# Changed places of modulation passes, attention values and an up-projection in a two-block transformer kernel

## The chip, the cores and the metric

The kernel is one program on one core of one Trainium2 chip. Its time is the device time of one launch in microseconds (us). The core has a matrix engine, TensorE (PE in the rows; PEld is its weight load), VectorE (DVE), ScalarE (ACT), GpSimd (POOL) and SyncE (SP), whose queue issues most loads. The engines run their own instruction streams and meet at semaphores.

## The reference

Two transformer blocks in float32 on 256 tokens of width 1024. The change lies in the first block:

```python
mod = silu(c) @ ada_w + ada_b                       # 6 * 1024 values
shift1, scale1, gate1, shift2, scale2, gate2 = split(mod, 6)
u = rms_norm(x, norm1_g) * (1 + scale1) + shift1
q_a, kc, vc, ksl, vsl, kwn, vwn, g_a, q_b, k_b, v_b, m_a, m_b = split(u @ w_in)
q_a = rms_norm(q_a per head, q_norm_g)
y_a = nsa_attention(q_a, ...) @ w_up_nsa            # 8 heads: compressed, selected, window
y_b = stick_breaking_attention(q_b, k_b, v_b) @ w_up_sb   # 8 heads
h = x + gate1 * ((sigmoid(m_a) * y_a + sigmoid(m_b) * y_b) @ w_out)
h = h + gate2 * (square(relu((rms_norm(h) * (1 + scale2) + shift2) @ mlp_w1)) @ mlp_w2)
```

Stick breaking weighs a key by `exp(log_sigmoid(z) + suffix sum of log_sigmoid(-z))`. The second block (SwiGLU, spatial gating, latent and memory attention, SwiGLU) isn't touched.

## The kernel before

All weights come as one stream of 128x128 chunks, eight to a slot of 512 KB, in the order in which PE uses them (`stream_chunks`). SP loads slots into a ring of six; a slot is loaded again when PE has given it back. Each slot is used in two parts for precision: ACT rounds it into one of four halves (`round_slot`, L1363), then DVE subtracts the rounded from the full value in place (`split_slot`, L1809). Neither has a queue for that of its own: `ahead(name)` stands in their programs and works up to four slots past the slot in which PE makes `name`. A projection (`project`, L685 through `mm`) makes a block of 128 outputs for 256 tokens: per 128 rows of weights three matmuls, so 24 for a full block over 1024 rows and 12 for a half one.

PSUM has eight banks. `plan_psum` gives each named result a bank, in turn within a list of names; `claim` makes PE wait until the result before in that bank has been read, and `full` and `evacuated` are the other engines' waits. `proj_names` and `later_proj_names` use banks 0 to 2 in rotation, `long_names` bank 7, and `selection_names` lists its banks one by one.

The order in time around the change is the order in which each engine's program is written. PE: the first projections; `ga`, `ks`, `kw`, `qa0` to `qa3`, each with the sum of squares of the one before; the compression of keys and values (`cmp_hid_k`, `cmp_hid_v`, narrow matmuls); the scores of the first two stick-breaking heads; eight times a gate block `ma0` to `ma7` with one stick-breaking head (`sb_logits(h)`), and after every second the values of a pair of heads (`sb_values(b)`, result `sbo0` to `sbo3`); then eight times a gate block `mb0` to `mb7` with the turning (transpose) of one head's weights (`nsa_turn(i)`, L1005), scores and values of pairs (`nsa_scores`, `nsa_values`); then the up-projections `up_nsa0`, `up_sb0` and so on with the memory keys, the mixing (`mix0` to `mix7`), the memory values and the first hidden block.

DVE has at the query norms: `ada_step`, `normalise("qa0")`, and so on for four blocks. `normalise` (L1838) reads the bank of a query block and so frees it: `qa3` holds bank 2, which `ma0` needs. At the compression it multiplies (`cmp_turned`, L1975) what ACT's tanh (L1523) gives, and frees bank 0 for `ma1`. In the gate blocks it makes a head's logits with the bias (`nsa_logits`, L2011), and after ACT's exponentials (`exps`, L1555) scales them (`nsa_scale`, L2030 to L2035). `split_output` (L1824 and L1825) reads an attention output in two parts. ACT loads a table set (`ACT_TABLE_LOAD`) where the kind of function changes.

A modulation pass (`ada_step`, L1865) multiplies 128 rows of `ada_w` (512 KB) by `silu(c)` and sums along the row: one block of 128 values of `mod`. 16 early passes make `shift1` and `scale1`; 32 follow in the order `gate1`, `shift2`, `scale2`, `gate2`. POOL loads their weights into a ring of three (`load_ada`, L1269), the next when a pass is done, from a queue in which it also loads the bias, stores the rounded memory rows (two times 1 MB) and loads them back. `ADA_BEFORE_SB`, `ADA_SB` (per stick-breaking head), `ADA_IN_UP` and `ADA_IN_MIX` say where the 32 passes stand in DVE's program. `gate1` must be ready for the mixing, `shift2` and `scale2` after it.

The weights of the gate blocks' heads lie in two buffers, `logit[:, 0]` and `logit[:, 1]` (`wide[:, 24:28]` and `wide[:, 28:32]`), an odd head in the first. The stick-breaking buffers are `sbw`, `wide[:, 16:28]`: an even head in the first six blocks, an odd one in the last six.

## Time and profile before

| | us |
|---|---|
| three runs | 1054.4, 1056.98, 1057.65 |
| median | 1056.98 |
| profiled execution, its own time | 1056.08 |
| its span, first to last instruction | 1054.4 |
| busy: PE, DVE, ACT, POOL | 1028.0, 806.0, 617.4, 49.2 |

The span and the execution's own time differ by 1.7 us, which lie around the kernel. A timeline row gives start, duration, engine, line, operation, what it writes and reads, how many instructions are merged, and in square brackets idle time of that engine just before, with the line that ended it. An average over the span says little here: PE is busy almost always, and what can be won are single stops of it.

### The profile page before, as it was taken

What the parts mean: (1) busy time and instruction counts of PE and PEld (TensorE: products, weight loads), DVE (VectorE), ACT (ScalarE), POOL (GpSimd) and SP (SyncE); (2) the same over time, 40 slices, a digit from 0 to 9 for tenths busy, and PEclk for the clock granted to TensorE, in tenths of its full rate; (3) what the DMA queues carried; (4) which work ended last, traced back from release to release, by engine and by line L of the source; (5) the groups of instructions that cost most, each with busy time, mean ns of one, the idle gap of its engine ahead of it and who ended that gap; (6) DMA issues with size and microseconds to landing.
All of it is one profiled execution on the core that took longest, in us unless ns stands there. A gap on an engine that the chain in (4) does not pass through costs nothing.

```text
span 1054.4 us, 18897 instructions
## 1 busy us (share of the span) xinstructions
PE 1028.0 (97%) x6878; PEld 932.6 (88%) x6878; DVE 806.0 (76%) x1480; ACT 617.4 (59%) x1147; POOL 49.2 (5%) x74
## 2 busy tenths in 40 slices
PE   6997989999999999999999999999999999999998
PEld 5997978998988888888888889899999998888887
DVE  6987877886998655588887878576867878888753
ACT  5485778545665544466655367696654466555532
POOL 1001100001110000000000010000000020000000
PEclk9998999999999999999999999999999999999999
DMA  9988763668776666666666664455444555666663
GB/s 363 403 313 303 231 206 123 196 196 271 273 224 191 189 189 191 181 185 194 184 195 186 185 187 151 154 147 173 124 138 125 167 170 180 186 193 186 193 185 117
DMA packets 58507, 209.46 MB, mean 199 GB/s; under 512 B 7055, under 2 KB 8463, under 8 KB 57912
## 3 DMA queue, kind: packets, MB, share of 16 engines
q1 hardware_dynamic: 52616, 185.24, 56.1%
q0 software_dynamic: 5808, 23.09, 6.2%
q8 instruction: 55, 0.90, 0.3%
q14 instruction: 28, 0.23, 0.1%
HBM read 205.14 MB, written 3.16 MB: 198 GB/s over the span
## 4 chain that ended last, share of the span: by engine, by line
PE 87%; DVE 5%; ACT 4%; DMA 2%; issue 1%; POOL 0%; ACTq 0%; DVEq 0%; SPq 0%; POOLq 0%
PE bank L685 86%; DVE ring_rounded L1809 2%; ACT rounded_rounded L1363 2%; DMA ada_ring<-in_ada 1%; DMA ring<-in_stream 1%; PE bank L1005 1%; ACT body L1555 1%; DMA x<-in_x_t 0%; DVE ada_ring L2124 0%; DVE body L2035 0%; ACT body_rounded L1412 0%; DVE part L2353 0%; DVE x L2094 0%; DVE x L2165 0%; DVE x L2164 0%
## 5 line engine op out<-in xcount | busy, mean ns | idle before, releaser
L685 PE MATMUL bank<-u_rounded,rounded_rounded 128*128 128x256 f32 (+1 forms) x2136 | 510.4, 331 | 6.4 <-DVE qa L1838 4.7
L1809 DVE TENSOR_TENSOR ring_rounded<-ring,rounded_rounded 128x1024 fp32r<-128x1024 f32 x326 | 397.2, 1225 | 119.0 <-ACT rounded_rounded L1363 112.5
L1363 ACT ACTIVATE rounded_rounded<-ring 128x1024 fp32r<-128x1024 f32 x326 | 341.9, 1054 | 103.2 <-PE bank L685 80.4
L685 PE MATMUL bank<-u_rounded,ring_rounded 128*128 128x256 f32 x1504 | 351.0, 281 | 0.0
L685 PEld LDWEIGHTS bank<-u_rounded,rounded_rounded 128*128 128x128 f32 x2136 | 332.7, 189 | 11.7 <-DVE qa L1838 4.9
L685 PE MATMUL bank<-body_rounded,rounded_rounded 128*128 128x256 f32 (+1 forms) x1296 | 321.9, 335 | 2.1 <-DVE body_rounded L2063 1.3
L685 PEld LDWEIGHTS bank<-u_rounded,ring_rounded 128*128 128x128 f32 x1504 | 284.2, 189 | 37.9
L685 PE MATMUL bank<-body_rounded,ring_rounded 128*128 128x256 f32 x952 | 217.2, 280 | 0.0
L685 PEld LDWEIGHTS bank<-body_rounded,rounded_rounded 128*128 128x128 f32 x1296 | 201.4, 188 | 4.2 <-DVE body_rounded L2063 1.7
L685 PEld LDWEIGHTS bank<-body_rounded,ring_rounded 128*128 128x128 f32 x952 | 178.9, 188 | 26.4
L1616 ACT ACTIVATE part<-bank 128x256 f32<-128x256 f32 x65 | 24.9, 384 | 81.1 <-PE bank L685 81.1
L1865 DVE CUSTOM_DVE_ANT_0 ada_ring<-ada_ring,ada_acc,cols 128x1024 f32<-128x1024 f32 x38 | 48.3, 1280 | 5.2 <-DMA ada_ring<-in_ada 5.2
L1312 POOL TENSOR_TENSOR turned<-turned 128x256 f32<-128x256 f32 x20 | 19.9, 995 | 575.8 <-ACT turned L1639 376.1
L2140 DVE TENSOR_TENSOR part<-bank,part 128x256 f32<-128x256 f32 x65 | 27.6, 424 | 18.4 <-ACT part L1616 18.4
L1555 ACT ACTIVATE body<-body,stats 128x128 f32<-128x128 f32 (+2 forms) x64 | 25.9, 406 | 18.0 <-DVE stats L2327 15.4
L1616 ACT ACTIVATE body<-bank 128x256 f32<-128x256 f32 x44 | 16.8, 382 | 33.1 <-PE bank L685 33.1
L1593 ACT ACTIVATE body_rounded<-body 128x256 fp32r<-128x256 f32 x76 | 31.2, 411 | 8.1 <-DVE body L2218 3.9
L2067 DVE TENSOR_TENSOR body_rounded<-body,body_rounded 128x256 fp32r<-128x256 f32 x76 | 31.8, 419 | 1.1 <-ACT body_rounded L1593 1.0
L685 PE MATMUL bank<-rounded_rounded,u_rounded 128*128 128x512 f32 (+1 forms) x96 | 28.6, 370 | 3.6 <-DVE u_rounded L1907 3.6
L2140 DVE TENSOR_TENSOR body<-bank,body 128x256 f32<-128x256 f32 x44 | 18.7, 424 | 14.6 <-ACT body L1616 14.6
L685 PE MATMUL bank<-body,mats 128*128 128x256 f32 (+1 forms) x82 | 19.8, 382 | 5.6 <-ACT body L1399 5.6
L1269 POOL DMA_DIRECT2D ada_ring<-in_ada x32 | 17.1, 534 | 152.1 <-DVE mod L1865 151.2
(268 smaller groups left out, 883.0 us busy)
## 6 DMA issues: line engine op xcount, KB each, us to landing
ring<-in_stream SPq DMA_DIRECT2D x328, 512.0 KB, 4.2
ada_ring<-in_ada POOLq DMA_DIRECT2D x32, 512.0 KB, 5.1
body<-in_ada SPq DMA_DIRECT2D x8, 512.0 KB, 9.4
ada_ring<-in_ada SPq DMA_DIRECT2D x6, 512.0 KB, 8.4
mem_parts_kept<-body_rounded POOLq DMA_DIRECT2D x2, 1024.0 KB, 7.0
body_rounded<-mem_parts_kept POOLq DMA_DIRECT2D x2, 1024.0 KB, 5.8
x<-in_x_t SPq DMA_DIRECT2D x2, 512.0 KB, 4.8
body<-in_mem_t SPq DMA_DIRECT2D x2, 512.0 KB, 7.1
```

Source lines behind the costliest of these rows:

```text
L685: return nc.tensor.matmul(out, lhs, rhs, start=start, stop=stop, skip_group_check=True)
L1005: return nc.tensor.transpose(ps[:, at_col:at_col + P], src, mat("ident"))
L1269: pool.dma_start(ada_ring[:, n % ADA_RING, :], ada[ADA_EARLY + n]).then_inc(ada_full[n % ADA_RING], 16)
L1312: ins = pool.tensor_tensor(row_squares[:, i, :], row_squares[:, i - 1, :], row_squares[:, i, :], ALU.add)
L1363: a(R(slot_round(q)), slot_weights(n), ACT.Copy).then_inc(slot_rounded, 1)
L1555: ins = a(dst, src, ACT.Exp, scale=-1.0 if i < 8 else 1.0, bias=stats[:, i % 2, 0, k:k + 1], accum_out=stats[:, i % 2, 1, k:k + 1])
L1593: a(R(hidden[:, i, :]), hidden_lo[:, i, :], ACT.Copy).then_inc(hidden_rounded, 1)
L1616: a(dst, bank(name)[:, T:2 * T], ACT.Copy).then_inc(half_copied, 1)
L1809: v.tensor_tensor(R(w), w, R(slot_round(q)), ALU.subtract).then_inc(slot_split, 1)
L1865: v.tensor_tensor_reduce(out=w, in0=w, in1=c_row, scale=0.5, scalar=col("ada_b", at), op0=ALU.mult, op1=ALU.add, accum_out=mod[:, at:at + ...
L2067: v.tensor_tensor(R(hidden_lo[:, i, :]), hidden_lo[:, i, :], R(hidden[:, i, :]), ALU.subtract).then_inc(hidden_ready, 1)
L2140: free(v.tensor_tensor(dst, bank(name)[:, 0:T], dst, ALU.add), name)
```

## The change

The results and the counts of all kinds of work stay as they are; the order and three places in memory change.

- Modulation passes: two stand before the split of the slots at `ks` (`ADA_IN_KEYS`), three before `qa0`, `qa1` and `qa2`, none before `qa3` and none behind it; one less in stick-breaking head 6 (14 passes before the up-projections instead of 16); one more in the up-projections and one more in the mixing. POOL issues the first two reloads ahead of the memory rows' stores.
- The last stick-breaking values (`sb_values(3)`) come behind `mb0`; their result goes to bank 1 instead of 7.
- DVE makes the logits of heads 0 and 1 in a row, before head 0's scaling. ACT takes head 0's exponentials ahead of stick-breaking head 7's, and its table load stands before the copy of `ma7`. Odd heads' weights go to `wide[:, 16:20]`.
- `up_sb0` comes before the last head's turn, its chunks are first in the stream, and `up_sb0` and `up_nsa0` use banks 0 and 2, `up_nsa1` bank 1.

```diff
@@ -52,8 +52,8 @@
 ADA_EARLY = 16
-ADA_SB = (2, 1, 1, 2, 1, 2, 1, 0)
-ADA_BEFORE_SB, ADA_IN_UP, ADA_IN_MIX = 6, (0, 2, 4), (0, 1, 2, 5, 6)
+ADA_SB = (2, 1, 1, 2, 1, 2, 0, 0)
+ADA_IN_KEYS, ADA_BEFORE_SB, ADA_IN_UP, ADA_IN_MIX = 2, 5, (0, 2, 4, 6), (0, 1, 2, 4, 5, 6)
 ADA_UP = ADA_BEFORE_SB + sum(ADA_SB) + ADA_RING
@@ -129,8 +129,11 @@
     for m in range(KD):
+        if m == 0:
+            stationary("w_up_sb", span(m * P), half)
         stationary("w_up_nsa", span(m * P), [span(b * HD, HD) + span((4 + b) * HD, HD) for b in range(4)])
-        stationary("w_up_sb", span(m * P), half)
+        if m:
+            stationary("w_up_sb", span(m * P), half)
         if m % 2 == 0:
@@ -286,8 +289,8 @@
 def later_proj_names():
-    out = []
-    for m in range(KD):
+    out = ["up_sb0", "up_nsa1", "up_nsa0", "up_sb1"]
+    for m in range(2, KD):
         out += [f"up_nsa{m}", f"up_sb{m}"]
@@ -316,7 +319,7 @@
-    out = [("sbz6", 1), ("sbz7", 2), ("ma5", 0), ("ma6", 0), ("ma7", 0)]
+    out = [("sbz6", 1), ("sbz7", 2), ("sbo3", 1), ("ma5", 0), ("ma6", 0), ("ma7", 0)]
     for i in range(8):
@@ -341,7 +344,7 @@
 def long_names():
-    return ["mem_ss", "qa1"] + [f"sbo{b}" for b in range(4)]
+    return ["mem_ss", "qa1"] + [f"sbo{b}" for b in range(3)]
@@ -455,6 +458,7 @@
         logit = flat(wide[:, 24:32, :]).rearrange("p (a b) -> p a b", a=2)
+        nsa_weights = [flat(wide[:, 28:32, :]), flat(wide[:, 16:20, :])]
@@ -1006,7 +1010,7 @@
                 pe.wait_ge(weights_ready, i + 1)
-                w = logit[:, 1 - i % 2, :]
+                w = nsa_weights[i % 2]
                 for t, c in enumerate("sw"):
@@ -1052,12 +1056,19 @@
                     nsa_scores(0)
+            project("mb0", KD, u_parts)
             sb_values(3)
+            def up_sb(m):
+                project(f"up_sb{m}", 4, (attn_b, attn_b_lo1), (lambda i: evacuated(pe, f"sbo{i}")) if m == 0 else None)
+
             for i in range(8):
-                project(f"mb{i}", KD, u_parts)
+                if i:
+                    project(f"mb{i}", KD, u_parts)
                 if i and i % 2 == 0:
                     nsa_values(i // 2 - 1)
+                if i == 7:
+                    up_sb(0)
                 nsa_turn(i)
@@ -1068,8 +1079,9 @@
                     sum_squares(f"mem_k{m // 2}", "ones")
-                project(f"up_sb{m}", 4, (attn_b, attn_b_lo1), (lambda i: evacuated(pe, f"sbo{i}")) if m == 0 else None)
-                if m == 0:
+                if m:
+                    up_sb(m)
+                else:
                     pe.wait_ge(loaded["mem_back"], 32)
@@ -1286,6 +1298,7 @@
                            ).then_inc(loaded["bias"], 16)
+            load_ada(ADA_RING, ADA_RING + ADA_IN_KEYS)
             pool.wait_ge(u_rounded, (ROW_MEM + 1) * KD)
@@ -1294,7 +1307,7 @@
                 pool.tensor_copy(bias_cmp[:, :, t, 0:seen], backwards(bias, (seen - 1) * CMP_STRIDE, seen, CMP_STRIDE)).then_inc(lines_ready, 1)
-            load_ada(ADA_RING, ADA_UP)
+            load_ada(ADA_RING + ADA_IN_KEYS, ADA_UP)
@@ -1511,9 +1524,27 @@
+            def exps(i, parts):
+                if i < 8:
+                    ahead(f"nsa{i}a")
+                    evacuated(act, f"nsa{i}a")
+                else:
+                    ahead(f"mla{i - 8}")
+                    act.wait_ge(logits_ready, i - 8 + 1)
+                for k, (src, dst) in parts.items():
+                    ins = a(dst, src, ACT.Exp, scale=-1.0 if i < 8 else 1.0, bias=stats[:, i % 2, 0, k:k + 1], accum_out=stats[:, i % 2, 1, k:k + 1])
+                ins.then_inc(weights_raw, 1)
+
+            def nsa_exp(i):
+                w = nsa_weights[i % 2]
+                at = [w[:, 0:128], w[:, 128:256], w[:, 256:512], w[:, 512:768], w[:, 768:768 + N_CMP], w[:, 784:784 + N_CMP]]
+                exps(i, {k: (s, s) for k, s in enumerate(at)})
+
             act.wait_ge(mem_stored, 32)
             sb_log(0)
             for h in range(8):
+                if h == 7:
+                    nc.scalar.preload_act_table_set("exp_and_others")
                 copy(gates[:, h, :], f"ma{h}")
@@ -1541,27 +1572,10 @@
                     sb_log(h + 1)
+                else:
+                    nsa_exp(0)
                 sb_exp(h)
-
-            def exps(i, parts):
...
-            nsa_exp(0)
-            nc.scalar.preload_act_table_set("exp_and_others")
             for i in range(8):
@@ -1924,6 +1938,9 @@
                 free(v.tensor_scalar(pair_q[:, b, :], bank(f"qb{b}")[:, b % 2 * T:(b % 2 + 1) * T], HD ** -0.5, None, ALU.mult), f"qb{b}")
+            for i in range(ADA_IN_KEYS):
+                ahead("ks", i + 1)
+                ada_step()
             ahead("ks")
@@ -1945,10 +1962,9 @@
             for b in range(4):
-                ada_step()
+                if b < ADA_BEFORE_SB - ADA_IN_KEYS:
+                    ada_step()
                 normalise(f"qa{b}", [qa[:, b, :]], "q_norm")
-            for _ in range(ADA_BEFORE_SB - 4):
-                ada_step()
@@ -2001,7 +2017,7 @@
                 h = i // 2 + 4 * (i % 2)
-                w, st = logit[:, 1 - i % 2, :], stats[:, i % 2, :, :]
+                w, st = nsa_weights[i % 2], stats[:, i % 2, :, :]
                 if i >= 2:
@@ -2044,10 +2060,10 @@
             nsa_logits(0)
+            nsa_logits(1)
             dve.wait_ge(gate_t_ready, TT)
             nsa_scale(0)
             split_output(attn_b[:, 3, :], attn_b_lo1[:, 3, :], "sbo3")
-            nsa_logits(1)
             for i in range(8):
                 if i < 6:
                     nsa_logits(i + 2)
```

The function `exps` and `nsa_exp` are moved as they are but for the buffer, and `nsa_scale` takes the new buffer too.

Three places in the order of instructions follow. The first is DVE at the query norms. ISA is a modulation pass with the read of its sum, `ring_rounded` a slot split. Before:

```order
L1838 SCALAR_TENSOR_TENSOR qa<-bank,cols,rinv 128x256
L1865 ISA ada_ring,mod<-ada_ring,ada_acc,cols 128x1024
L1865 ISA mod 128x1
L1809 TENSOR_TENSOR ring_rounded<-ring,rounded_rounded 128x1024
L1838 SCALAR_TENSOR_TENSOR qa<-bank,cols,rinv 128x256
L1865 ISA ada_ring,mod<-ada_ring,ada_acc,cols 128x1024
L1865 ISA mod 128x1
L1809 TENSOR_TENSOR ring_rounded<-ring,rounded_rounded 128x1024
L1838 SCALAR_TENSOR_TENSOR qa<-bank,cols,rinv 128x256
L1865 ISA ada_ring,mod<-ada_ring,ada_acc,cols 128x1024
```

The same place now, from the pass before `qa2`:

```order
L1879 ISA ada_ring,mod<-ada_ring,ada_acc,cols 128x1024
L1879 ISA mod 128x1
L1823 TENSOR_TENSOR ring_rounded<-ring,rounded_rounded 128x1024
L1852 SCALAR_TENSOR_TENSOR qa<-bank,cols,rinv 128x256
L1823 TENSOR_TENSOR ring_rounded<-ring,rounded_rounded 128x1024
L1852 SCALAR_TENSOR_TENSOR qa<-bank,cols,rinv 128x256
```

Between the last two query norms a slot split is left and no pass.

The second place is ACT at the end of stick breaking: `body<-bank1` and `body<-bank2` are the exponentials of stick-breaking heads 6 and 7, `body<-bank0` first the copy of `ma7` and then the tanh of `mb0`, `body,stats` the exponentials of head 0. Before:

```order
L1512 ACTIVATE body<-bank1 128x384
L1363 ACTIVATE rounded_rounded_50<-ring 128x1024
L1425 ACTIVATE body<-bank0 128x256
L1512 ACTIVATE body<-bank2 128x384
L1555 ACTIVATE body,stats<-body,stats 128x128 x2
L1555 ACTIVATE body,stats<-body,stats 128x256 x2
L1555 ACTIVATE body,stats<-body,stats 128x15 x2
L1564 ACT_TABLE_LOAD
L1363 ACTIVATE rounded_rounded_50<-ring 128x1024
L1567 ACTIVATE body<-bank0 128x256
```

Now:

```order
L1525 ACTIVATE body<-bank1 128x384
L1547 ACT_TABLE_LOAD
L1376 ACTIVATE rounded_rounded_50<-ring 128x1024
L1438 ACTIVATE body<-bank0 128x256
L1535 ACTIVATE body,stats<-body,stats 128x128 x2
L1535 ACTIVATE body,stats<-body,stats 128x256 x2
L1535 ACTIVATE body,stats<-body,stats 128x15 x2
L1525 ACTIVATE body<-bank2 128x384
L1376 ACTIVATE rounded_rounded_50<-ring 128x1024
L1581 ACTIVATE body<-bank0 128x256
```

Head 7's exponential moved behind six others, the table load ahead of two instructions.

The third place is DVE from the scaling of head 0 on. Before:

```order
L2033 TENSOR_TENSOR stats<-stats,gate_t 128x6
L2035 TENSOR_SCALAR body<-body,stats 128x128 x2
L2035 TENSOR_SCALAR body<-body,stats 128x256 x2
L2035 TENSOR_SCALAR body<-body,stats 128x15 x2
L1809 TENSOR_TENSOR ring_rounded_49<-ring,rounded_rounded_50 128x1024
L1824 CAST body_rounded_54<-bank7 128x256
L1825 TENSOR_TENSOR body_rounded_54<-bank7,body_rounded_54 128x256
L2011 ISA body,stats<-bank6,body 128x256
```

Now:

```order
L2049 TENSOR_TENSOR stats<-stats,gate_t 128x6
L2051 TENSOR_SCALAR body<-body,stats 128x128 x2
L2051 TENSOR_SCALAR body<-body,stats 128x256 x2
L2051 TENSOR_SCALAR body<-body,stats 128x15 x2
L1823 TENSOR_TENSOR ring_rounded_49<-ring,rounded_rounded_50 128x1024 x2
L1838 CAST body_rounded_54<-bank1 128x256
L1839 TENSOR_TENSOR body_rounded_54<-bank1,body_rounded_54 128x256
L2027 ISA body,stats<-bank4,body 128x256
```

The logits of head 1 (`bank6`) have moved ahead of the scaling, so those of head 2 (`bank4`) follow; two slots are split here instead of one, and the output comes from bank 1.

## Rows read from the trace of the kernel before

**Rows 1.** The page, part 1: busy us, share of the span, instructions.
```profile
PE 1028.0 (97%) x6878; PEld 932.6 (88%) x6878; DVE 806.0 (76%) x1480; ACT 617.4 (59%) x1147; POOL 49.2 (5%) x74
```
**Rows 2.** Timeline of DVE, 64 to 100 us: start, us, what, [idle before, releaser].
```profile
68.10 1.23 DVE L1809 TENSOR_TENSOR ring_rounded<-ring,rounded_rounded 128x1024 fp32r<-128x1024 f32 x1 [1.40 <-ACT rounded_rounded L1363]
...
88.80 0.48 DVE L1838 SCALAR_TENSOR_TENSOR qa<-bank,cols,rinv 128x256 f32<-128x256 f32 x1
94.18 1.28 DVE L1865 CUSTOM_DVE_ANT_0 ada_ring<-ada_ring,ada_acc,cols 128x1024 f32<-128x1024 f32 x1 [4.91 <-DMA ada_ring<-in_ada]
```
**Rows 3.** The chain that ended last, 60 to 240 us: start, us, what.
```profile
84.84 9.32 DMA ada_ring<-in_ada
...
97.06 5.50 PE bank L685 x24
```
**Rows 4.** Timeline of PE, 96 to 106 us: the first matmuls of `ma0` and `ma1`.
```profile
97.06 0.80 PE L685 MATMUL bank<-u_rounded,rounded_rounded 128*128 128x256 f32 x2 [4.67 <-DVE qa L1838]
...
105.29 0.51 PE L685 MATMUL bank<-u_rounded,rounded_rounded 128*128 128x256 f32 x2 [0.40 <-DVE cmp_turned L1975]
```
**Rows 5.** Windows: us, busy PE, PEld, DVE, ACT, POOL, granted clock, DMA share, GB/s.
```profile
97.00:105.20 8.20, 7.83 (x39) 7.25 (x39) 6.21 (x13) 2.51 (x7) 1.06 (x2) 0.66 0.78 261
146.00:151.00 5.00, 2.86 (x24) 2.43 (x24) 3.57 (x18) 2.37 (x10) 0.00 (x0) 1.00 0.34 134
```
**Rows 6.** Timeline of PE, 141 to 155 us, from `sb_values(3)` on.
```profile
141.75 0.87 PE L685 MATMUL bank<-body,pair_v 128*64 128x256 f32 x8 [0.63 <-issue]
...
146.06 0.28 PE L1005 MATMUL bank<-mats,body 128*15 128x128 f32 x1 [0.40 <-DVE body L2035]
147.97 0.94 PE L1005 MATMUL bank<-mats,body 128*15 128x128 f32 x7 [1.64 <-DVE body_rounded L1825]
149.36 1.72 PE L685 MATMUL bank<-kcat,qa 64*128 64x256 f32 x16 [0.45 <-DVE stats L2011]
151.01 0.50 PE L685 MATMUL bank<-u_rounded,rounded_rounded 128*128 128x256 f32 x2
...
153.96 1.04 PE L1005 MATMUL bank<-mats,body 128*15 128x128 f32 x8
```
**Rows 7.** Timeline of DVE, 144 to 152 us: end of `sbo3`'s split, head 2's logits.
```profile
147.50 0.42 DVE L1825 TENSOR_TENSOR body_rounded<-bank,body_rounded 128x256 fp32r<-128x256 f32 x1
...
150.60 0.42 DVE L2011 CUSTOM_DVE_ANT_0 body<-bank,body 128x256 f32<-128x256 f32 x1 [1.39 <-PE bank L685]
```
**Rows 8.** Timeline of PE, 185 to 189 us: turn of head 7, last values.
```profile
186.00 1.05 PE L1005 MATMUL bank<-mats,body 128*15 128x128 f32 x8
187.92 1.30 PE L685 MATMUL bank<-turned,vcat 128*64 128x256 f32 x12 [0.88 <-DVE body_rounded L1825]
```
**Rows 9.** Timeline of ACT, 90 to 96 us: the rounding ahead of `ma0`'s copy.
```profile
94.55 1.06 ACT L1363 ACTIVATE rounded_rounded<-ring 128x1024 fp32r<-128x1024 f32 x1 [0.47 <-DMA ring<-in_stream]
```
**Rows 10.** Timeline of ACT, 136 to 145 us.
```profile
137.49 1.06 ACT L1363 ACTIVATE rounded_rounded<-ring 128x1024 fp32r<-128x1024 f32 x1 [1.54 <-PE bank L685]
...
141.16 0.49 ACT L1512 ACTIVATE body<-bank 128x384 f32<-128x384 f32 x1 [0.61 <-PE bank L685]
...
143.99 1.28 ACT L1564 ACT_TABLE_LOAD   x1
```
**Rows 11.** Timeline of ACT, 185 to 189 us: the tanh of `mb7`.
```profile
186.42 0.35 ACT L1567 ACTIVATE body<-bank 128x256 f32<-128x256 f32 x1
```
**Rows 12.** Timeline of DVE, 218 to 243 us: splits behind m = 6 and before `mix4`.
```profile
223.76 2.36 DVE L1809 TENSOR_TENSOR ring_rounded<-ring,rounded_rounded 128x1024 fp32r<-128x1024 f32 x2 [1.20 <-ACT rounded_rounded L1363]
...
241.93 1.23 DVE L1809 TENSOR_TENSOR ring_rounded<-ring,rounded_rounded 128x1024 fp32r<-128x1024 f32 x1 [1.43 <-ACT rounded_rounded L1363]
```
**Rows 13.** Timeline of POOL, 230 to 243 us: the load behind the second gathered square.
```profile
236.26 0.56 POOL L1269 DMA_DIRECT2D ada_ring<-in_ada  x1 [0.30 <-POOL turned L1312]
```
**Rows 14.** DMA issues, 64 to 67 and 73 to 77 us: KB, us to landing.
```profile
ring<-in_stream SPq DMA_DIRECT2D x2, 512.0 KB, 6.1
...
ring<-in_stream SPq DMA_DIRECT2D x2, 512.0 KB, 3.5
```

15 lines of the change are left out of this document (1 added, 14 removed).

## The prediction

> **What bounds the kernel now.** I read the page first: TensorE (PE) is busy 97% of the span of 1054.4 us, so only its stops, and stretches at a lower clock, can be won [rows 1]. Then I took PE in order of time and looked for idle time before a row, and last the engine that ends each such stop. Three stops lie where the change edits.
>
> The first is at the query norms. VectorE (DVE) normalises qa2 at 88.80, then takes a modulation pass whose weights have not landed: idle 4.91 us, pass at 94.18 [rows 2]. Behind the pass stand a slot split and the norm of qa3, and only that norm frees bank 2 for `ma0`. The chain of waits shows it whole: the load is issued at 84.84 and takes 9.32 us, then comes the pass, then PE at 97.06 [rows 3]. PE has stood for 4.67 us by then [rows 4], so it was ready at 92.39. After that stop the granted clock of PE is 0.66 on average from 97 to 105.2 [rows 5]: most of the stretch runs at 1.2 GHz, the lower of its two levels. The 24 matmuls of `ma0` take 5.50 us [rows 3], where a projection of the same 24 at 2.4 GHz takes 153.96 − 151.01 = 2.95 us [rows 6].
>
> The second place is the passage from stick-breaking to the gate blocks. PE stands 0.63, 0.40, 1.64 and 0.45 us in 8 us [rows 6]: for head 7's exponential on ScalarE (ACT), for the scaled weights of head 0, for bank 7 (the split of `sbo3`, DVE's row at 147.50 [rows 7]) and for the logits of head 1. The third is 0.88 us before the last values, with a turn ending ahead of it [rows 8].
>
> **The change, part by part.**
>
> *Passes off the query norms.* Six passes stood here. Three stay, ahead of `qa0` to `qa2`; two move earlier, between the slot splits at the keys; one, like one of stick-breaking head 6, moves later (below). At the keys DVE is idle 1.40 us before a split, waiting for ACT's rounding [rows 2]; two passes of 1.28 us [rows 2] make one split about 1.1 us late, which the next such wait takes back, so I price them at nothing. If that cover were gone, it would be 1.1 us at most. Their ring slots are then reloaded before the 1 MB stores of the memory rows. No pass stands before qa3's norm any more: DVE goes 88.80 + 0.48 + a split of 1.23 + 0.48 = 91.0 us, before PE asks at 92.39. `ma0` starts there and ends at 92.39 + 2.95 = 95.34 if the clock stays at 2.4 GHz, as it does through stops of 0.4 to 1.64 us (the second of [rows 5]).
>
> What is late next? In the kernel before, `ma0` ends at 97.06 + 5.50 = 102.56 and `ma1` starts at 105.29 [rows 3, 4]: 2.73 us for ACT's copy, its table load, the tanh of the compressed blocks and DVE's product, which frees bank 0. That chain stays. ACT also rounds a weight slot at 94.55 for 1.06 us, after a wait for that slot's load [rows 9], so the copy starts at 95.61, not 95.34. `ma1` then starts at 95.61 + 2.73 = 98.34: **105.29 − 98.34 = 7.0 us gained**, of which about 2.5 are clock. Lower end 4.4 (the clock falls all the same), upper end 7.2 (that rounding costs nothing).
>
> *Last stick-breaking values beside a gate block, and two heads' logits in a row.* PE ended its work for head 7 at 141.75 − 0.63 = 141.12. If nothing held it, it would now do `mb0` (2.95), the values of heads 6 and 7 (0.87), the turn of head 0 (about 1.0), scores (151.01 − 149.36 = 1.65) and `mb1` (2.95), and stand at the turn of head 1 at 150.5 instead of 153.96 [rows 6]. That would be 3.4 us. Who holds it? ACT now takes head 0's exponentials before head 7's. It had stood 0.61 us for PE and worked 0.4 on head 7 before them [rows 10], so they come 1.0 us earlier, the weights too, and the turn of head 0 can start at 146.06 − 1.0 = 145.1 [rows 6]; PE arrives at 144.9. Head 7's exponential ends near 143.4, before PE wants it at 144.1. ACT's table load of 1.28 us leaves the place behind the exponentials and goes where ACT stood 1.54 us [rows 10]: hidden. Bank 7 isn't used by `sbo3` any more (1.64 gone), and head 1's logits follow head 0's at once (0.45 gone). The dropped pass frees DVE 1.28 us ahead of them.
>
> The new bound is DVE. After head 0's weights (145.0) it splits two slots, not one, since the values now lie a slot further on (2 × 1.23), and `sbo3` (2 × 0.42) [rows 2, 7]: 148.3. Head 2's logits start then. From their start to the turn of head 1 went 153.96 − 150.60 = 3.36 us [rows 6, 7]; the queue is the same, so the turn comes at 151.6 less the overlaps of these rows (0.1 each, 0.2 in all) = 151.4. **Gain 153.96 − 151.4 = 2.5 us**; PE stands 0.9 us there. Ends: 3.4 (DVE not late) and 1.0 (only bank 7's stop goes, and DVE's extra split is paid).
>
> *Up-projection by the last head.* `up_sb0` needs bank 0, which `mb7` has just filled and ACT empties at 186.42 + 0.35 = 186.77 [rows 11]; `mb7` ended at 186.00 [rows 8]. So PE stands 0.8 us before `up_sb0`, does half a projection (1.45), turns head 7, and then stands again, some 0.3, while ACT copies the turned blocks. The old stop of 0.88 goes, 1.1 takes its place: **loss 0.2 us**. Ends: gain 0.9 (ACT earlier than now), loss 1.1.
>
> *Passes moved later.* One in the up-projections (m = 6) and one before `mix4`. DVE stands 1.20 us behind m = 6 and 1.43 us before `mix4`'s split [rows 12], so each is covered to within 0.1. The pass before `mix4` takes a load issued behind the second gathered square; that issue stood at 236.26 [rows 13]. With the 3.5 us of an undisturbed slot [rows 14] it lands in time; with 9.32 [rows 3] the load would land at 245.6, DVE would be some 4 us late, and idle times like those of [rows 12], one per block, would take back most of it. Price taken 0, far end a loss of 2.
>
> Sum: −7.0 − 2.5 + 0.2 = **−9.3 us**, against the profiled execution's 1056.08 us: 1046.8. The median of the runs is 1056.98, 0.9 higher; with it 1047.7. I predict **1047.2 us**.
>
> **The rivals.**
>
> *The early loads crowd the weight slots* (chance 0.10). Two loads of 512 KB now run around 67 to 72 us. A slot issued from 64 to 67 lands in 6.1 us, one issued from 73 to 77 in 3.5 [rows 14]: other traffic costs a slot 2.6 us. ACT rounds slots in order and in between makes the inverse norms, so such a delay would reach the query norms, and PE: 2.6 us back, 1049.8. Against it: the early loads are issued behind the 1 MB load of the bias rows on the same queue, so they may start only when that crowd is gone. The Trainium skill, DMA: Bandwidth & Descriptors, section Queues, rings and completion order, says that each DMA engine takes turns between its queues packet by packet, so that loads of one queue would slow the other's; by that rule the sum is 1049.8 and not 1047.2. No row of this trace has these two queues alone together, so the rule has neither been borne out nor refuted here.
>
> *The clock falls all the same* (0.07). PE does only narrow matmuls before `ma0`, and two stops of about half a microsecond follow it. Then `ma0` costs 5.50 again: 2.55 us back, 1049.8.
>
> *The passage gains nothing* (0.09). DVE's extra split and an order in which head 7's exponential waits behind six others move the stops instead of ending them. Then 1047.2 + 2.5 = 1049.7.
>
> *The change doesn't reach PE at `ma0`* (0.03): something else, such as the slot that ACT waited for at 94.55 [rows 9], holds PE to 97. Only 2.3 us are left: about 1054.2, no measurable difference. Against it: PE's releaser is DVE's norm, by name [rows 4].
>
> *Slower* (0.02). Every short stop that stays or is made (0.6 before the compression, 0.5 and 0.6 around the gates' turn, 0.9 at head 1, 0.8 and 0.3 at the end) throws PE to 1.2 GHz, each for as long as after 97 us, at 2.55 us each. From five such falls on (12.8) the gain of 9.3 is lost by more than 3.2 us, 0.3%, which is about what a measurement of this kernel can tell from no change; with six, 1047.2 + 15.3 = 1062.5. Against it: from 146 to 151 PE was busy 2.86 of 5.00 us and the granted clock stayed 1.00 [rows 5]. The Trainium skill, TensorE: Matmul & The Clock Gate, section A second HAM failure mode: psum-queue depth-cycling, speaks for this rival: frequent small idle times between groups of matmuls made the clock of another kernel swing between its levels. The trace here disagrees so far.
>
> **How the numbers follow.** The forecast has 0.69. All cases but the last two are faster by over 3.2 us, and a little is left for a sum of late costs: faster 0.95, same 0.03, slower 0.02. The range runs from 1044.6 (both stops at PE's own limit, the last one hidden, with a low run) to 1050.6, which takes in each of the first three rivals alone.
>
> **What would show it.** In the profile after: no idle time of DVE for `ada_ring` around qa3's norm; `ma0` about 4.7 us earlier and at a granted clock of 1.00; `ma1` about 7 us earlier, with an idle time before it near 0.6 from the compression's product; no stop for bank 7; a stop of about 1 us before the turn of head 1; one of about 0.8 us before `up_sb0`, released by ACT; everything from the mixing on equal and shifted by 9.3. The prediction is wrong if PE stands for DVE or for a weight slot in the first 90 us, if the clock row shows a fall between 90 and 110 us, or if a new stop appears from `mix4` to the first hidden block.

## The result and the profile after

The change runs in 1049.1 us (median of six runs, 1048.36 to 1050.37), the kernel before in 1056.88 us in the same session; the ratio is 0.9926, 95% interval [0.9912, 0.9939]: 7.8 us faster. Predicted were 1047.2 us, range 1044.6 to 1050.6. The profiled execution of the change took 1050.37 us, the slowest of its six, and its span is 1048.7 us, 5.7 less than before.

I split both spans at places that every version has. The start of each stretch is a row of the timeline: DVE's row that scales the queries (before 62.79), PE's first matmul of `ma1` (105.29) and of the turn of head 1 (153.96), and PE's first 512-wide matmul, where `mem_v` begins (248.83).

| stretch, us | before | change | difference | predicted |
|---|---|---|---|---|
| start to scaled queries | 62.79 | 62.06 | −0.73 | 0 |
| to `ma1` | 42.50 | 36.98 | −5.52 | −7.0 |
| to the turn of head 1 | 48.67 | 46.40 | −2.27 | −2.5 |
| to `mem_v` | 94.87 | 95.44 | +0.57 | +0.2 |
| to the end of the span | 805.57 | 807.82 | +2.25 | 0 |

The page's first part hardly moves, against [rows 1]:

```profile
PE 1025.6 (98%) x6878; PEld 930.6 (89%) x6878; DVE 806.6 (77%) x1480; ACT 617.4 (59%) x1147; POOL 50.1 (5%) x74
```

**Query norms.** DVE's timeline of the change, in answer to [rows 2]: no pass and no wait stands before the last norm.

```profile
87.39 0.48 DVE L1852 SCALAR_TENSOR_TENSOR qa<-bank,cols,rinv 128x256 f32<-128x256 f32 x1
87.78 1.22 DVE L1823 TENSOR_TENSOR ring_rounded<-ring,rounded_rounded 128x1024 fp32r<-128x1024 f32 x1
89.03 0.48 DVE L1852 SCALAR_TENSOR_TENSOR qa<-bank,cols,rinv 128x256 f32<-128x256 f32 x1
```

PE's timeline, in answer to [rows 4]: `ma0` starts with no stop, 6.1 us earlier than before, but a new stop of 1.86 us comes behind it, before the gates' turn.

```profile
90.96 0.51 PE L689 MATMUL bank<-u_rounded,rounded_rounded 128*128 128x256 f32 x2
...
96.50 0.59 PE L689 MATMUL bank<-mats,turned 24*128 24x24 f32 x4 [1.86 <-ACT body L1438]
...
99.04 0.63 PE L689 MATMUL bank<-u_rounded,rounded_rounded 128*128 128x256 f32 x2
```

ACT's timeline says why (before: [rows 9], idle 0.47): the copy that empties `ma0`'s bank stands behind the rounding of a slot, and that slot is still on its way.

```profile
95.03 1.06 ACT L1376 ACTIVATE rounded_rounded<-ring 128x1024 fp32r<-128x1024 f32 x1 [2.30 <-DMA ring<-in_stream]
95.99 0.36 ACT L1438 ACTIVATE body<-bank 128x256 f32<-128x256 f32 x1
```

The windows of the change (columns as in [rows 5]) show the clock before, in and after that stop. It is at 2.4 GHz through `ma0` and at 1.2 GHz from 98 to 100.

```profile
90.00:94.00 4.00, 4.00 (x35) 3.65 (x33) 2.28 (x4) 1.90 (x5) 0.00 (x0) 1.00 1.01 406
94.60:96.50 1.90, 0.04 (x2) 0.03 (x1) 0.39 (x1) 1.46 (x3) 0.00 (x0) 1.00 0.90 364
...
98.00:99.00 1.00, 1.00 (x6) 1.00 (x5) 0.82 (x5) 0.92 (x5) 0.00 (x0) 0.50 0.00 0
99.00:100.00 1.00, 1.00 (x7) 1.00 (x6) 0.91 (x7) 0.99 (x2) 0.00 (x0) 0.50 0.00 0
```

The DMA issues from 84 to 86 us (KB each, us from issue to landing), where an undisturbed slot takes 3.5 us [rows 14]:

```profile
ada_ring<-in_ada POOLq DMA_DIRECT2D x1, 512.0 KB, 10.7
ring<-in_stream SPq DMA_DIRECT2D x1, 512.0 KB, 9.2
```

**Passage and last head.** PE's timeline, in answer to [rows 6] and [rows 8]: one stop of 0.44 us at the turn of head 1 in place of four, and two around `up_sb0` in place of one.

```profile
145.44 1.05 PE L1009 MATMUL bank<-mats,body 128*15 128x128 f32 x8 [0.44 <-DVE body L2051]
...
178.33 0.50 PE L689 MATMUL bank<-body_rounded,rounded_rounded 128*128 128x256 f32 x2 [0.77 <-ACT body L1581]
...
181.38 1.52 PE L689 MATMUL bank<-turned,vcat 128*64 128x256 f32 x16 [0.49 <-ACT turned L1588]
```

**Mixing.** DVE's timeline with the passes ahead of `mix4`, `mix5` and `mix6`, and then the split that `mem_v` needs:

```profile
232.92 1.29 DVE L1879 CUSTOM_DVE_ANT_0 ada_ring<-ada_ring,ada_acc,cols 128x1024 f32<-128x1024 f32 x1 [0.39 <-DMA ada_ring<-in_ada]
...
236.26 1.28 DVE L1879 CUSTOM_DVE_ANT_0 ada_ring<-ada_ring,ada_acc,cols 128x1024 f32<-128x1024 f32 x1
...
242.53 1.28 DVE L1879 CUSTOM_DVE_ANT_0 ada_ring<-ada_ring,ada_acc,cols 128x1024 f32<-128x1024 f32 x1 [2.92 <-DMA ada_ring<-in_ada]
...
243.94 1.22 DVE L1823 TENSOR_TENSOR ring_rounded<-ring,rounded_rounded 128x1024 fp32r<-128x1024 f32 x1
```

The load of the last of them is this row of POOL, and it lands 7.4 us later:

```profile
235.10 0.56 POOL L1281 DMA_DIRECT2D ada_ring<-in_ada  x1 [0.30 <-POOL turned L1325]
```

PE then has two stops that the kernel before doesn't have, at the second part of `mem_v` and at the first block of the hidden layer:

```profile
245.22 0.50 PE L689 MATMUL bank<-rounded_rounded,body_rounded 128*128 128x512 f32 x1 [1.40 <-DVE ring_rounded L1823]
...
256.40 0.36 PE L689 MATMUL bank<-u_rounded,rounded_rounded 128*128 128x256 f32 x1 [0.81 <-issue]
```

### The profile page after: what moved, and what is told of

It is laid out like the page before. It is cut to its first block, busy times and chain, and to the rows that moved or that the text cites. A ratio compares the mean times of both kernels' runs of the same rounds, so it can differ in the third digit from the quotient of the medians.

```text
span 1048.7 us, 18897 instructions
## 1 busy us (share of the span) xinstructions
PE 1025.6 (98%) x6878; PEld 930.6 (89%) x6878; DVE 806.6 (77%) x1480; ACT 617.4 (59%) x1147; POOL 50.1 (5%) x74
## 4 chain that ended last, share of the span: by engine, by line
PE 84%; DVE 7%; issue 3%; ACT 3%; DMA 2%; POOL 1%; SPq 0%; DVEq 0%; ACTq 0%; POOLq 0%
PE bank L689 83%; DVE ring_rounded L1823 3%; DMA ring<-in_stream 2%; ACT rounded_rounded L1376 1%; PE bank L1009 1%; DMA ada_ring<-in_ada 1%; ACT body L1535 1%; DVE ada_ring L1879 0%; POOL turned L1325 0%; DVE ada_ring L2140 0%; DVE body L2051 0%; DVE body_rounded L2079 0%; DVE part L2092 0%; DVE part L2369 0%; ACT turned L1587 0%
## 5 line engine op out<-in xcount | busy, mean ns | idle before, releaser
L2156 DVE TENSOR_TENSOR part<-bank,part 128x256 f32<-128x256 f32 x65 | 27.6, 424 | 17.8 <-ACT part L1630 17.7
```

Source lines behind the costliest of these rows:

```text
L2156: free(v.tensor_tensor(dst, bank(name)[:, 0:T], dst, ALU.add), name)
```

## The experiments

Each kernel was timed beside the kernel before; "own time" is that of its profiled execution. The edits are shown in part, with ... where lines are left out. The kernel before had medians of 1057.0, 1055.88, 1056.68 and 1056.54 us in the four sessions.

### The first part alone

```diff
 # on the kernel before
-ADA_BEFORE_SB, ADA_IN_UP, ADA_IN_MIX = 6, (0, 2, 4), (0, 1, 2, 5, 6)
+ADA_IN_KEYS, ADA_BEFORE_SB, ADA_IN_UP, ADA_IN_MIX = 2, 5, (0, 2, 4, 6), (0, 1, 2, 5, 6)
...
+            load_ada(ADA_RING, ADA_RING + ADA_IN_KEYS)
...
-            load_ada(ADA_RING, ADA_UP)
+            load_ada(ADA_RING + ADA_IN_KEYS, ADA_UP)
...
+            for i in range(ADA_IN_KEYS):
+                ahead("ks", i + 1)
+                ada_step()
...
-                ada_step()
+                if b < ADA_BEFORE_SB - ADA_IN_KEYS:
+                    ada_step()
                 normalise(f"qa{b}", [qa[:, b, :]], "q_norm")
-            for _ in range(ADA_BEFORE_SB - 4):
-                ada_step()
```

> The kernel before with the first part of the change alone: passes off the query norms (two at the keys, three ahead of qa0 to qa2, one at m = 6 of the up-projections); passage, up_sb0 and mixing as before. Theory (parts add up: this part gives what ma1's earlier start shows, 6.3 us less some 1.4 of start-up luck in that profile): 5 to 6 us faster, ratio 0.994 to 0.995; ma0 within 0.3 us of qa3's norm, the slot that ACT rounds ahead of ma0's copy lands late (1.5 us or more of PE idle before the gates' turn), a clock below 1.00 for 2 to 4 us after it, and no stop of PE around the mixing's end. Rival (the keys' part was only luck of the start-up): under 4 us faster. Rival (late slots were made by the whole of the change, not by these loads): PE idle under 0.5 us before the gates' turn, ma1 7 us earlier.

Measured: 1052.15 us, ratio 0.9962 [0.9948, 0.9975]; own time 1051.6. By the medians that is 4.9 us faster, just short of the 5 to 6 expected. The stretch to `ma1` is 36.30 us: 6.2 gained. The slot was not late and the clock stayed up, so that part of the expectation is a miss. PE stands elsewhere, before the compression, for the norm of qa2, which comes later. PE's timeline:

```profile
90.35 2.22 PE L685 MATMUL bank<-ring,turned 128*35 128x64 f32 x32 [1.17 <-DVE qa L1839]
```

The stretch from `ma1` to the turn of head 1 is 50.27 us, 1.6 more than before, although the stops of the old passage are the same four. The windows around them (the four stops begin at 135 and end at 143):

```profile
140.00:144.00 4.00, 1.91 (x13) 1.49 (x15) 3.08 (x15) 1.37 (x7) 0.00 (x0) 0.95 0.39 155
144.00:148.00 4.00, 4.00 (x26) 3.81 (x23) 2.47 (x18) 4.00 (x15) 0.00 (x0) 0.63 0.04 8
```

The clock fell behind the old passage here, and didn't in the profile of the kernel before: this profile can't say what the first part does to the passage. From `mem_v` to the end it takes 805.52 us, as before: the 2.25 us lost there by the change don't come with this part.

### The change without its first part

```diff
-ADA_IN_KEYS, ADA_BEFORE_SB, ADA_IN_UP, ADA_IN_MIX = 2, 5, (0, 2, 4, 6), (0, 1, 2, 4, 5, 6)
+ADA_IN_KEYS, ADA_BEFORE_SB, ADA_IN_UP, ADA_IN_MIX = 0, 6, (0, 2, 4, 6), (0, 1, 2, 5, 6)
...
-                if b < ADA_BEFORE_SB - ADA_IN_KEYS:
-                    ada_step()
+                ada_step()
                 normalise(f"qa{b}", [qa[:, b, :]], "q_norm")
+            for _ in range(ADA_BEFORE_SB - 4):
+                ada_step()
```

> The changed kernel without its first part: six passes at the query norms as before, and no pass ahead of mix4 (one at m = 6 of the up-projections in its place); passage and up_sb0 as changed. Theory: PE stands 4.7 us for qa3's norm again; the passage gives 2.8 us, up_sb0 takes 0.5, nothing is lost at the mixing: 2.3 us faster than before, ratio 0.998. Rival (the passage's gain exists only because PE and DVE arrive there in another order, thanks to the first part): under 1 us, ratio 0.999 or above.

Measured: 1052.88 us, ratio 0.996 [0.9947, 0.9974]; own time 1055.13, the slowest of its six. By the medians that is 4.1 us faster, where 2.3 were expected: a miss, and the profiled execution doesn't show where the rest lies. PE stands 5.95 us for qa3's norm, not 4.7. To `ma1` 42.96 us, from there to the turn of head 1 45.83 (before 48.67: 2.8 gained), to `mem_v` 95.45 (0.6 lost), to the end 805.49. In the trace the passage gives 2.8 us without the first part, so the rival falls.

### `up_sb0` back in its place

```diff
-                if i == 7:
-                    up_sb(0)
...
-                if m:
-                    up_sb(m)
-                else:
+                up_sb(m)
+                if m == 0:
```

> The changed kernel with up_sb0 back at its old place, behind the first up-projection of the other branch. Theory: the stops of 0.8 and 0.5 us go, one of about 0.9 before the last values is back; 0.3 to 0.5 us faster than the change, ratio to before 0.992. Rival (up_sb0 by the last head is worth its place): 0.2 us or more slower than the change. In either case the stops of the mixing's end (1.4 us for a split of DVE, 0.8 us before w1_0) stay.

Measured: 1047.8 us, ratio 0.9922 [0.9904, 0.994]; own time 1045.56. One stop of 0.88 us before the last values; turn of head 1 to `mem_v` 94.93 us, 0.5 less than in the change. But the stops of the mixing's end, expected to stay, are gone too (`mem_v` to the end 805.38): here the load for the pass of `mix6` landed in 5.1 us. It also went out sooner. GpSimd's product just ahead of it took 0.74 us, against 1.74 in the change, where VectorE's pass of `mix4` had begun just before that product (DVE's row at 232.92 above). GpSimd's timeline of the change, then of this run:

```profile
233.06 1.74 POOL L1325 TENSOR_TENSOR turned<-turned 128x256 f32<-128x256 f32 x1 [1.46 <-ACT turned L1412]
```

```profile
230.61 0.74 POOL L1319 TENSOR_TENSOR turned<-turned 128x256 f32<-128x256 f32 x1 [1.46 <-ACT turned L1406]
```

The load went out 3.06 us behind the one before it here, and 4.06 in the change. In this run the pass of `mix4` had waited 0.86 us for its own load and began 0.33 us after the product did. The same long product (1.67 to 1.76 us) stands in all four profiles that have the stop at `mem_v`; it is 0.73 in the kernel before.

### `mix4`'s pass among the up-projections

```diff
-ADA_IN_KEYS, ADA_BEFORE_SB, ADA_IN_UP, ADA_IN_MIX = 2, 5, (0, 2, 4, 6), (0, 1, 2, 4, 5, 6)
+ADA_IN_KEYS, ADA_BEFORE_SB, ADA_IN_UP, ADA_IN_MIX = 2, 5, (0, 2, 4, 5, 6), (0, 1, 2, 5, 6)
```

> The changed kernel with the pass of mix4 taken at m = 5 of the up-projections; five passes in the mixing at 0, 1, 2, 5, 6 as before. Theory (the third load of the mixing, for the pass of mix6, is issued behind a square at 235 and lands 7.4 us later; DVE waits 2.9 us for it, and PE 1.4 us and perhaps the 0.8 before w1_0): both stops go, 1.4 to 2.2 us faster than the change, ratio to before 0.9905 to 0.9915, no idle time of DVE for the ring of passes in the mixing. Rival (the stops there come from the kernel arriving 8 us earlier relative to something else): they stay, ratio 0.9925. Rival (a pass at m = 5 makes DVE late for the norm of the memory keys there): a new stop of PE before mem_k2 or up_nsa6, gain under 1 us.

Measured: 1049.06 us, ratio 0.9927 [0.9913, 0.994]; own time 1049.04. Both stops are gone (`mem_v` to the end 805.15), and no new one came at the mixing. But the median isn't lower than the change's, where 1.4 to 2.2 us were expected: in the runs the edit gained nothing that can be told. In its trace the start (64.33 to the scaled queries) took 2.3 us more than in the change's, and nothing in the edit touches it.

### The change once more

No edit.

> The changed kernel once more, unaltered, to see what of its first profile is the kernel's and what that execution's. Theory (the late slot ahead of ma0's copy, 1.9 us of PE and a slower clock after it, and the stops of 1.4 and 0.8 us around the mixing's end come from loads that land in 7 to 9 us in one execution and in 5 to 7 in another): at least one of the two is missing from this profile, while the stops of 0.4 (head 1's turn), 0.8 (up_sb0) and 0.5 (last values) are the same to 0.05; ratio 0.992 to 0.994. Rival (they belong to this kernel, and taking up_sb0 or the pass of mix4 elsewhere removed them): both are there, within 0.3 us.

Measured: 1047.84 us (1046.34 to 1050.9), ratio 0.9921 [0.9903, 0.9938]; own time 1050.9, again the slowest of six. The late slot is missing. The other stops are there; PE's timeline:

```profile
91.10 2.21 PE L689 MATMUL bank<-ring,turned 128*35 128x64 f32 x32 [1.18 <-DVE qa L1852]
...
245.65 0.50 PE L689 MATMUL bank<-rounded_rounded,body_rounded 128*128 128x512 f32 x1 [1.37 <-DVE ring_rounded L1823]
...
256.82 0.36 PE L689 MATMUL bank<-u_rounded,rounded_rounded 128*128 128x256 f32 x1 [0.82 <-issue]
```

So the late slot is that execution's; the mixing's stops came in both profiles of the change. To `ma1` it took 37.12 us all the same, for the keys took longer. DVE's timeline has the scaled queries and the last split of the keys 9.99 us apart:

```profile
62.83 0.76 DVE L1940 TENSOR_SCALAR body<-bank 128x256 f32<-128x256 f32 x2 [1.36 <-PE bank L689]
...
72.82 1.23 DVE L1823 TENSOR_TENSOR ring_rounded<-ring,rounded_rounded 128x1024 fp32r<-128x1024 f32 x1 [1.71 <-ACT rounded_rounded L1376]
```

In the kernel before these two rows are 8.25 us apart. In every profile the norm of qa2 follows that split by 17.8 us: what is lost here arrives there whole.

The loss comes from a weight slot, and not from the two passes. ACT rounds a slot at 68.79 as soon as it has landed:

```profile
68.79 1.06 ACT L1376 ACTIVATE rounded_rounded<-ring 128x1024 fp32r<-128x1024 f32 x1 [1.76 <-DMA ring<-in_stream]
```

The DMA issues from 58 to 59 us, of this profile and then of the kernel before:

```profile
ring<-in_stream SPq DMA_DIRECT2D x1, 512.0 KB, 10.6
```

```profile
ring<-in_stream SPq DMA_DIRECT2D x1, 512.0 KB, 8.9
```

It was issued at 58.14, 7.2 us before the first pass at the keys (65.30).

### Three loads later

```diff
+            evacuated(pool, "ma0")
             load_ada(ADA_RING + ADA_IN_KEYS, ADA_UP)
```

> The changed kernel with the three modulation loads of the stretch from 83 to 98 us issued only once ma0's bank has been emptied (their passes come at 102 and later). Theory (slots land in 7 to 9 us there because they share the DMA engines with two 1 MB stores and these 1.5 MB): a slot issued at 84 to 90 lands in under 6 us, ACT doesn't wait for one ahead of ma0's copy, PE doesn't stand before the gates' turn, clock 1.00; the same time as the change in executions without the late slot, 2 to 3 us less than its first profile; the median 0 to 1 us lower. Rival (the stores are what delays the slots): landings stay at 7 us or more. Rival (loads so late miss their passes in stick-breaking): DVE idle for the pass ring over 1 us at 100 to 108, slower by 1 us or more.

Measured: 1048.63 us, ratio 0.9925 [0.9904, 0.9945]; own time 1049.74. The DMA issues from 86 to 88 us hold the slot that ACT waits for ahead of `ma0`'s copy, where the change had 9.2 for it:

```profile
ring<-in_stream SPq DMA_DIRECT2D x1, 512.0 KB, 4.8
```

The stretch to `ma1` is 34.99 us, 7.5 less than before. The two 1 MB stores are still there, so it was the three loads beside them: this slot lands in 4.7 to 5.0 us in all four profiles with the edit, and in 7.2 to 9.2 in the ten without. The end of this profile gives part of the gain back: behind the stops of 0.49 and 0.81 us at the mixing's end the clock falls, and from `mem_v` on it takes 808.8 us. Windows:

```profile
256.00:264.00 8.00, 7.92 (x39) 6.53 (x40) 8.00 (x15) 4.32 (x7) 0.63 (x2) 0.79 0.49 177
```

### Passes at the keys one split later

```diff
             for i in range(ADA_IN_KEYS):
-                ahead("ks", i + 1)
+                ahead("ks", i + 2)
```

> The changed kernel with each of the two passes at the keys one slot split later, so that they stand ahead of the splits at which DVE waits 1.4 and 1.7 us in the kernel before. Theory (where they stand now, both run ahead of those waits, and the first pushes a split by 1.0 us down the chain to the query norms, which shows as 1.17 us of PE before the compression of the values): from the scaled queries to the last split of the keys 8.2 us as before the change, not 9.1; PE idle before the compression of the values at most 0.6; 0.8 to 1.0 us faster than the change. Rival (the waits there are for slots still landing, and the early pass loads lengthen those landings wherever the passes stand): 9.1 us and 1.17 us stay, no faster.

Measured: 1049.85 us, ratio 0.994 [0.9922, 0.9958]; own time 1053.14, the slowest of its six. The keys' stretch is 7.44 us and PE doesn't wait for a norm, as expected. But the edit didn't do that: the slot issued at 57.88 landed in 8.1 us (10.6 in the run of the change once more), and 4.07 us behind its landing came the last split. And the kernel isn't faster, for the slot ahead of `ma0`'s copy is late. ACT's timeline, then PE's:

```profile
95.59 1.06 ACT L1376 ACTIVATE rounded_rounded<-ring 128x1024 fp32r<-128x1024 f32 x1 [2.24 <-DMA ring<-in_stream]
```

```profile
97.06 0.59 PE L689 MATMUL bank<-mats,turned 24*128 24x24 f32 x4 [1.81 <-ACT body L1438]
```

`ma1` comes after 36.63 us, with the clock down again. In each of the eight profiles that have the first part and the three loads where the change has them, PE stands for one of the two, the late norm (0.74 to 1.20 us) or the late slot (1.32 to 1.86 us), and never for both.

### Three edits, then four, and four less one

The first run has the keys' passes later, `mix4`'s pass at m = 5 and `up_sb0` back in its place, the second also the later loads; so the two differ in those loads alone.

> Three edits on the changed kernel together: passes at the keys one split later, mix4's pass at m = 5 of the up-projections, up_sb0 back in its old place. Theory: 1.0 for the first, 0.5 for the last, and the second takes away a stop that comes only in some executions (0 to 2 us): median 1.5 to 2.5 us below the change, ratio to before 0.990 to 0.991. Rival (what a part gives at its place is taken back by a later wait, as with the clock): ratio 0.992 or above.

Measured: 1048.19 us, ratio 0.9925 [0.9909, 0.9942]; own time 1048.31. Nothing lost at the mixing (805.46), but PE stands 1.32 us before the gates' turn with the clock down behind it, and `ma1` comes after 36.41 us. The forecast of 1.5 to 2.5 us below the change was missed (0.992 was the rival's bound), and the rival was right.

> Four edits on the changed kernel: passes at the keys one split later, the three loads of 83 to 98 us after ma0's bank is emptied, mix4's pass at m = 5 of the up-projections, up_sb0 in its old place. Theory: from the scaled queries to the last split of the keys at most 8.0 us, slots of 84 to 90 land in under 5.5 us, no stop before the gates' turn or at the mixing's end, clock 1.00 from 90 to 270; ma1 34.5 to 35.2 us after the scaled queries (42.5 before, 37.0 in the change's first profile); median 1045 to 1046.5, ratio 0.989 to 0.991. Rival (another slot or ACT's own chain holds the same place): ma1 no nearer than 36, ratio 0.992.

Measured: **1046.22 us**, ratio 0.9905 [0.9884, 0.9925]; own time 1045.6. To `ma1` 34.75 us, to the turn of head 1 45.81, to `mem_v` 95.14, to the end 805.62. Against the run with three edits the later loads give 1.7 us before `ma1`, and 1.4 us behind it, where the clock stays up; the medians, of two sessions, differ by 2.0. Windows:

```profile
90.00:105.00 15.00, 14.60 (x121) 13.41 (x119) 9.88 (x26) 13.78 (x29) 2.64 (x5) 1.00 0.66 236
240.00:270.00 30.00, 29.90 (x189) 26.07 (x188) 25.53 (x42) 20.71 (x34) 2.11 (x4) 1.00 0.69 234
```

> The same but for up_sb0, which stays by the last head as in the change. Theory: stops of 0.77 and 0.49 us in place of one of 0.88 and PE otherwise the same, so 0.4 us slower than the kernel with all four edits (within what a comparison of runs can tell); from the turn of head 1 to the end of the first pair of up-projections 0.4 us longer in the trace. Rival (the stop between mixing and mem_v comes with up_sb0's place, since the run with the old place had none though the pass of mix4 was kept): here, without that pass, it comes back, 0.5 us or more before mem_v.

Measured: 1046.02 us, ratio 0.9906 [0.9885, 0.9927]; own time 1046.0. Turn of head 1 to `mem_v` 95.67 us against 95.14: the 0.5 us are in the trace, and the runs can't tell them. No stop at the mixing's end (805.55), so it needs the pass of `mix4`.

> The kernel with all four edits but the first: passes at the keys where the change has them. Theory: from the scaled queries to the last split of the keys 7.9 to 10 us by execution (8.4 on average), 0.5 to 1 us slower than with all four, by a stop of PE of up to 1.2 us before the compression of the values. Rival (what the keys give is taken back by the slot behind them, as in the run with that edit alone): no slower than with all four, ratio 0.989 to 0.991 for both.

Measured: 1046.75 us, ratio 0.9908 [0.9887, 0.9929]; own time 1046.98. Keys 7.96 us, to `ma1` 35.09 (34.75 with the edit): 0.3 us, not told apart by the runs, as the rival said. The slot that sets the keys' stretch landed in 8.5 us here and in 8.1 with the edit.

### The mixing's loads earlier

GpSimd issues two loads behind the first square, one each behind the next two.

```diff
-gather_squares(ROW_1, "mix", lambda i: load_ada(ADA_MIX + i - 1, ADA_MIX + i))
+gather_squares(ROW_1, "mix", lambda i: load_ada(ADA_MIX + min(i, 4) - (i == 1), ADA_MIX + min(i + 1, 4)))
```

> The changed kernel with its passes where they are, but GpSimd issues two loads behind the first gathered square of the mixing and one behind the second and third, so that the load for the pass ahead of mix6 goes out one square (some 3 us) earlier. Theory (that one load, issued at 235.1 for a pass due at 239.6, makes DVE 2.9 us late and PE stand 1.4 and 0.8 us): DVE idle for it under 0.5 us, neither stop, and the time from the start of mem_v to the end of the profile 805.5 us, as in every profile without the stops, not 807.8; median 0 to 2.3 us below the change. Rival (five slots and four passes in 15 us are too much for the DMA engines whatever the order): the stop moves or stays, 807 us or more from mem_v to the end.

Measured: 1049.6 us, ratio 0.9926 [0.9908, 0.9945]; own time 1051.48. The wait has moved to the pass of `mix4`. DVE's timeline:

```profile
235.81 1.28 DVE L1879 CUSTOM_DVE_ANT_0 ada_ring<-ada_ring,ada_acc,cols 128x1024 f32<-128x1024 f32 x1 [2.06 <-DMA ada_ring<-in_ada]
```

`mem_v` isn't held any more, the first hidden block is (0.67 us), and the clock falls behind it:

```profile
260.00:264.00 4.00, 3.98 (x19) 3.58 (x19) 4.00 (x7) 1.73 (x3) 0.53 (x1) 0.62 0.34 114
```

From `mem_v` to the end: 807.72 us. Loads pulled together also slow each other: those issued at 229.5 landed in 7.2 us, a slot of 230 to 232 in 8.2. The rival was right for this order: the wait moved and the loss stayed. It isn't shown that no order would do, for with `up_sb0` undone the same passes cost nothing.

## Why the prediction was right, and where it was not

The sign, the range and the main mechanism held: 7.8 us gained by the medians, 9.3 forecast. That the total came within 2 us is in part luck, for two terms were short by 1.5 and by 2.3 us in the profiles. By terms:

**Passes off the query norms: 7.0 predicted, 5.5 and 5.4 in the two profiles of the change.** The stop of 4.67 us went, as predicted, and `ma0` ran at 2.4 GHz in both; no version with this part had it otherwise. What is missing lies in two places.
- "What is late next?" is the step that failed. I took the slot rounding at 94.55 for fixed. With PE early that slot comes late: it was 1.86 us of PE and a clock fall in one profile. With three loads out of its way it landed in 4.8 instead of 9.2 us and the stretch gave 7.5 us, over the predicted 7.0 (and over its upper end of 7.2).
- The start of the chain isn't fixed either. I took the norm of qa2 at 88.80 from one profile. It follows the last split of the keys by 17.8 us, and that split follows the landing of one slot, issued between 57.4 and 59.6 us, by 4.0 to 4.2 us, in all fourteen profiles. The slot took 9.8 to 10.6 us in four (the first part alone, `mix4`'s pass moved, the change once more, the mixing's loads earlier), where the keys' stretch is 9.08 to 9.99 us, and 8.1 to 9.0 in the other ten, where it is 7.42 to 8.41. In the second profile of the change this is 1.74 us of the stretch, which accounts for the 1.6 that are missing there. In the kernel before, by its rows, DVE would only have waited that much less than its 4.91 us [rows 2].

"I price them at nothing", of the two passes at the keys, held. Where the slot came soon, the last wait for ACT shrank from 1.71 to between 0.33 and 1.18 us, as reckoned; where it came late, the passes ran while DVE would have waited for ACT anyway. The expectations of "Passes at the keys one split later" and of the runs built on it put a late landing down to the passes; the four profiles with that edit have short keys because their slot landed in 8.1 to 8.6 us.

The rival of crowded slots had the mechanism, and it cost time at another place. At 67 to 72 us, where the two early loads are, a slot issued at 69 to 72 did take 5.5 to 7.5 us in the twelve profiles with these loads, and 3.7 and 4.2 in the two without, but ACT never waited for it. It struck at 84 to 95, where three loads follow two stores. For that crowd the rule that I quoted from the Trainium skill (DMA: Bandwidth & Descriptors, Queues, rings and completion order: DMA engines take turns between queues) fits the trace in what it would lead to: GpSimd's loads slow SyncE's slots, 9.2 us for a slot with them and 4.8 without. The taking of turns itself no row shows.

**Passage: 2.5 predicted, 2.8 measured** (45.80 to 45.95 us in all nine profiles of the new passage whose clock didn't fall, against 48.67). The stop at the turn of head 1 is 0.44 and not 0.9 us.

**`up_sb0` by the last head: loss of 0.2 predicted, 0.5 measured** (95.14 against 95.67 us with and without the edit, all else equal). The stop before it was 0.77 for 0.8; that before the last values 0.49 for 0.3.

**Passes moved later: "Price taken 0", measured 2.25 and 2.29 us.** This step failed too. I followed one load, that of `mix4`, and it was nearly in time (0.39 us of DVE). But a pass more moves every later load of the mixing: the one for `mix6` had 7.7 us from issue to use before (issued at 239.01, used at 246.74, no wait) and has 4.5 in the change (235.10 to 239.61, where DVE begins to wait), while landings there take 7.4. A part of the lost time is GpSimd's longer product ahead of that load (1.74 us for 0.74). The named far end, a loss of 2, was the right one. That the loss needs this pass is shown, and that the pass is not enough for it too: six profiles have it; five lose 2.2 to 3.8 us from `mem_v` on (the clock's falls there included), one (`up_sb0` undone) nothing; the other eight, the kernel before among them, all take 805.2 to 805.6 us.

**The clock.** The rival that the clock falls all the same at `ma0` fell. Falls did come behind other stops, and not wherever there were such stops: behind the gates' turn in three profiles with this part, behind the old passage in one, after the mixing in three. Each cost 1.3 to 1.9 us, an estimate by the length of its stretch against that of undisturbed profiles, both less their stops. What the Trainium skill reports of short idle times between matmuls (TensorE: Matmul & The Clock Gate, A second HAM failure mode: psum-queue depth-cycling), which I set aside by one row of the trace, is partly borne out: the same four stops, 0.40 to 1.64 us in 8 us, left the clock at 1.00 in one profile (the kernel before) and threw it to 0.63 in another (the first part alone).

**What stays open.** The profiles' terms add up to −5.7 and −5.2 us, the medians to −7.8 and −8.0. Both profiled executions of the change were the slowest of six. So its other executions probably lose less, at the mixing or by late slots; that is argued and not shown. It would also say why the kernel with `mix4`'s pass moved has no lower median (1049.06) though its trace has no stop. That `up_sb0`'s old place went with no stop at the mixing is seen in one profile only; its rows show the load going out a microsecond sooner and landing in 5.1 us for 7.4, and whether `up_sb0`'s place or that execution did this is open.

## What to carry to other kernels

When a wait is removed, look at what the engine meets next, and at the load behind that: the gain here ends at a weight slot whose landing depends on who else is loading, and issuing three loads some 10 us later gave 1.7 us more before `ma1`. Before a longer stretch is put down to an edit, compare when the load that it waits for was issued: here it was issued before the edited instructions ran, and the edit made to win back that time could not. When an item is added to a ring, follow every later load of that ring to its use, and not only the first. The version with all four edits takes 1046.22 us, ratio 0.9905 [0.9884, 0.9925], against 0.9926 and 0.9921 for the change; the intervals overlap, so that it beats the change is likely and not shown.

## What was not expected of the hardware

A slot of 512 KB landed in 3.5 and in 9.2 us within 11 us of the same profile (issued at 75.72 and 85.83 in the change). One slot, issued near 58 us with the same instructions before it, landed in 8.1 to 10.6 us by execution. A product of 128x256 on GpSimd took 0.73 or 0.74 us at its shortest, and 1.67 to 1.76 beside a VectorE pass and split, of which the split took 1.75 or 1.76 instead of 1.22. The stops just before don't tell whether the granted clock falls: behind the same four stops, in the same order of work, it was 1.00 in the kernel before and 0.63 in the kernel with the first part alone. Between 12 and 24 us it fell in all fourteen profiles, for longer in some than in others (granted clock from 16 to 20 and from 20 to 24 us: 0.64 and 1.00 with `up_sb0` undone, 0.50 and 0.74 with `mix4`'s pass moved). The scaled queries came at 62.11 us in the first of these and at 64.33 in the second, with nothing changed before them.
